# A new order in the k, v and r projections of an RWKV-7 / attention decoder, and a new beginning of its scan

## The chip, the cores and the metric

The kernel runs on one core of a Trainium2 chip. The metric is the device time of one execution in microseconds (us). Its engines are TensorE (PE; PEld is its weight load), VectorE (DVE), ScalarE (ACT), GpSimd (POOL) and SyncE (SP, which here only issues DMAs). Each runs its own instructions in program order; between engines there are semaphores only.

## What is computed

One step of a two-layer decoder trunk: 1024 prompt tokens and 8 sample tokens (1032 columns), model width 1024, 16 heads of 64. Layer 0 is an RWKV-7 mixer with its MLP, layer 1 windowed attention with its MLP. The change is in layer 0's mixer:

```
xr, xk, xv = h + (prev - h) * mix[...]           # prev: h one token earlier
r, k, v = xr @ w_r, xk @ w_k, xv @ w_v
kk = k * k_k, normalised per head;  k = k * (1 + (a - 1) * k_a)
state = state * w_t + (state @ a_t) b_t + v_t k_t   # a_t = -kk, b_t = kk * a; per token and head
y = state @ r_t;  bonus = sum(r * k * r_k) * v
```

The decay w and the gates a and g come from a stage before (scr_L, scr_A, scr_G in device memory).

## The kernel before, in words

Everything is stored channel-first: 8 row blocks of 128 channels by 1032 columns. The scan works on chunks of C = 64 tokens (16 chunks), so the projections also prepare, per chunk and head, the scaled rows At, Bt, Kt, Rt and the inverse T of a triangular system M.

**stage_kvr** makes k, v, r in 24 panels p of 128 output channels: k is p 0 to 7, v 8 to 15 (V0 = 8), r 16 to 23 (R0 = 16). A weight panel is loaded by SP (`weights`), rounded to a high part on ACT (`high`, L2052) and split on POOL (`wL`, L1891). PE then does, for each of 3 column slots, 8 row blocks times three products (high-high, low-high, high-low; L2015 to L2017): 72 matmuls of 344 columns. Panels 7, 8, 15 and 16 run `by_block` (L2031), row block outermost, since the operand changes there from x_k to x_v and from x_v to x_r: as soon as block b has been used (`s_used`), ACT may overwrite its high part (`used`, L1397), DVE its low part (`low`, L1401; `s_lo`). The mixed operand itself (`Blend`) is made ahead, one of 16 blocks at a time: `load` (ACT's DMA queue; it waits for mix b−2), `keep` (ACT, L1384), `mix` (DVE, L1392 and L1393). Between its slots PE does small work (`between`): for k block q the per-head sums of squares (`squares`, L1906) after slot 0 of panel q+1 and the systems (L1918) after slot 1 of panel q+2; for v the transposes to token order (`turn`, L1932, L1934), which ACT copies (`turned`, L2107, L2109) and SP stores; for r the bonus sums (`sums`, L1944).

The order of ACT within panel p is written out: square, high of the next panel, decays, keep, inverse_root (L2090, L2092), the loads, turned, then `copies` (L2061 for k, L2067 for v), which free PE's accumulators for the next panel. DVE does for k block q chain_a (needs scr_A's block, loaded by `load_A` on SP), chain_b, chain_c (at(q) is its last result), and the mask of q−1 (L2234); then the forward substitution of the 32 by 32 corners of all systems, two halves g of 30 steps with two instructions each (`forward`, L2246, L2248), with some mixes set between the steps (`aside`); then the 8 blocks of r (`scaled`, L2267; `bonus`, L2281) and the transposed corners (`turn_corners`, L2259). PE finishes T in panels 20 to 22 (`left` L1963, `right` L1975). SP issues in its own written order: in panel p weights of p+2, the three stores of k block p−1 (L1746 to L1750), L of p+1 (L1741), A of p (L1735), M of p−2 (L1754); later M by rows into the solve, T out and back in (`load_X`), and for r a store, the wait for its landing and the next load, for two buffers (`load_rL`, `load_rV`). `first_chunks` loads part of the scan's first operands (BK0, W0). The stage ends when SP has seen all its stores land; then comes a barrier of all engines.

**stage_scan** starts by loading AR (At and Rt of two chunks), Z (the T's) and W (values) on SP. PE turns the sample columns (`smp.turn`), ACT copies and stores them and loads them back by head (`spread`, `vectors`), DVE clears Y, ysq and Yt (2048, 512 and 2048 columns). Then come `grams` (L2566), `by_token` (L2582), `values_in`, and the 16 chunks of about 10 us each.

## Time and profile before

| | us |
|---|---|
| median of 3 runs | 2873.45 |
| lowest, highest | 2868.9, 2877.31 |
| the profiled execution | 2874.99 |
| its span in the profile | 2873.2 |
| PE, DVE, ACT, POOL busy | 2642.3, 1204.4, 961.9, 544.3 |

The profile is of one execution. PE is busy for 92% of its span. Matmuls are pipelined, so their busy times overlap and their starts tell the pace. A row of the timeline begins with start and duration; in brackets stands the time for which the engine was idle before, and what released it.

### The profile page before, as it was taken

What the parts mean: (1) busy time and instruction counts of PE and PEld (TensorE: products, weight loads), DVE (VectorE), ACT (ScalarE), POOL (GpSimd) and SP (SyncE); (2) the same over time, 40 slices, a digit from 0 to 9 for tenths busy, and PEclk for the clock granted to TensorE, in tenths of its full rate; (3) what the DMA queues carried; (4) which work ended last, traced back from release to release, by engine and by line L of the source; (5) the groups of instructions that cost most, each with busy time, mean ns of one, the idle gap of its engine ahead of it and who ended that gap; (6) DMA issues with size and microseconds to landing.
All of it is one profiled execution on the core that took longest, in us unless ns stands there. A gap on an engine that the chain in (4) does not pass through costs nothing. (4 is left out here: it accounts for less than half of the span.)

```text
span 2873.2 us, 48859 instructions
## 1 busy us (share of the span) xinstructions
PE 2642.3 (92%) x20648; PEld 2487.2 (87%) x20648; DVE 1204.4 (42%) x2171; ACT 961.9 (33%) x1817; POOL 544.3 (19%) x347
## 2 busy tenths in 40 slices
PE   4989878989958999999999999897999999999998
PEld 2768768878858899999999998786989999999998
DVE  5346686249967421211212252666562122121223
ACT  4446523324435421311202343556442021130221
POOL 1121211103330112121221312110212222222230
PEclk7999989989978999999999999999899999999999
DMA  8867659788673122222222222211211111111121
GB/s 321 325 238 236 206 192 266 202 210 194 168 234 94 59 89 88 74 88 89 74 88 89 87 76 71 65 28 39 84 42 51 45 45 52 45 45 52 45 67 60
DMA packets 375329, 332.04 MB, mean 116 GB/s; under 512 B 105688, under 2 KB 344988, under 8 KB 368046
## 3 DMA queue, kind: packets, MB, share of 16 engines
q1 hardware_dynamic: 353404, 288.22, 33.4%
q10 hardware_dynamic: 15986, 20.69, 2.3%
q0 software_dynamic: 5728, 20.06, 1.9%
...
q14 instruction: 47, 0.39, 0.0%
...
## 5 line engine op out<-in xcount | busy, mean ns | idle before, releaser
L531 POOL TENSOR_TENSOR wL<-raw,wH 128x1024 fp32r<-128x1024 f32 x120 | 288.0, 2400 | 1298.7 <-ACT wH L655 1298.7
L552 PE MATMUL t_acc<-oneH,wH 128*128 128x344 f32 x1488 | 483.5, 325 | 11.8 <-DVE oneL L899 5.8
L554 PE MATMUL t_acc<-oneH,wL 128*128 128x344 f32 x1488 | 478.4, 321 | 0.0
L553 PE MATMUL t_acc<-oneL,wH 128*128 128x344 f32 x1488 | 478.0, 321 | 0.0
L552 PE MATMUL t_acc<-twoH,wH 128*128 128x344 f32 x1392 | 449.2, 323 | 7.0 <-DVE twoL L874 4.8
L554 PE MATMUL t_acc<-twoH,wL 128*128 128x344 f32 x1392 | 445.9, 320 | 0.0
L553 PE MATMUL t_acc<-twoL,wH 128*128 128x344 f32 x1392 | 445.4, 320 | 0.0
L824 DVE SCALAR_TENSOR_TENSOR X<-t_acc,mod,X 128x344 f32<-128x344 f32 (+1 forms) x240 | 137.5, 573 | 615.7 <-PE t_acc L554 594.3
L904 DVE TENSOR_TENSOR t_g<-t_g 128x344 f32<-128x344 f32 x192 | 99.4, 518 | 553.2 <-ACT t_g L675 553.2
L552 PEld LDWEIGHTS t_acc<-oneH,wH 128*128 128x128 f32 x1488 | 281.9, 189 | 26.1 <-issue 10.1
L655 ACT ACTIVATE wH<-raw 128x1024 fp32r<-128x1024 f32 x120 | 126.5, 1054 | 507.6 <-PE t_acc L554 507.6
L553 PEld LDWEIGHTS t_acc<-oneL,wH 128*128 128x128 f32 x1488 | 282.4, 190 | 0.6
L554 PEld LDWEIGHTS t_acc<-oneH,wL 128*128 128x128 f32 x1488 | 282.3, 190 | 0.0
L552 PEld LDWEIGHTS t_acc<-twoH,wH 128*128 128x128 f32 x1392 | 262.3, 188 | 20.0 <-issue 11.2
L553 PEld LDWEIGHTS t_acc<-twoL,wH 128*128 128x128 f32 x1392 | 262.7, 189 | 0.1
L554 PEld LDWEIGHTS t_acc<-twoH,wL 128*128 128x128 f32 x1392 | 262.6, 189 | 0.0
L675 ACT ACTIVATE t_g<-t_acc 128x344 f32<-128x344 f32 x192 | 87.8, 457 | 508.0 <-PE t_acc L554 508.0
L2015 PE MATMUL kvr_acc<-hxH,kvr_wH 128*128 128x344 f32 x480 | 162.5, 339 | 10.7 <-PEq L122 7.3
L2016 PE MATMUL kvr_acc<-hxL,kvr_wH 128*128 128x344 f32 x480 | 156.6, 326 | 0.0
L2017 PE MATMUL kvr_acc<-hxH,kvr_wL 128*128 128x344 f32 x480 | 156.5, 326 | 0.0
L552 PE MATMUL t_acc<-twoH,oneH 128*128 128x344 f32 x336 | 114.0, 339 | 30.6 <-DVE twoL L899 29.9
L1891 POOL TENSOR_TENSOR kvr_wL<-kvr_raw,kvr_wH 128x1024 fp32r<-128x1024 f32 x22 | 58.6, 2665 | 324.4 <-ACT kvr_wH L2052 324.4
...
## 6 DMA issues: line engine op xcount, KB each, us to landing
...
```

Source lines behind the costliest of these rows:

```text
L531: pool.tensor_tensor(low, raw_of(w), high.bitcast(F32), ALU.subtract).then_inc(s_low, 1)
L552: pe.matmul(out, high[:, k, :], h[:, k, third[t]], start=(k == 0), stop=False)
L553: pe.matmul(out, high[:, k, :], l[:, k, third[t]], start=False, stop=False)
L554: return pe.matmul(out, low[:, k, :], h[:, k, third[t]], start=False, stop=(k == DB - 1))
L655: act.activation(place(kind, p)[0], raw_of(w), ACT.Copy).then_inc(s_high, 1)
L675: act.activation(gsq[:, i % 3, :], acc[u % 4][:, 0:TT], ACT.Relu).then_inc(s_relu, 1)
L824: ins = dve.scalar_tensor_tensor(out=x, in0=acc[u % 4][:, 0:z - a], scalar=gate[:, m, 0:1], in1=x, op0=ALU.mult, op1=ALU.add)
L904: dve.tensor_tensor(x, x, x, ALU.mult).then_inc(s_g, 1)
L1891: pool.tensor_tensor(wL[:, p % 2], raw[:, p % 2], wH[:, p % 2].bitcast(F32), ALU.subtract).then_inc(s_low, 1)
L2015: pe.matmul(out, wH[:, s, b, :], net.HH[:, b, t], start=(b == 0), stop=False)
L2016: pe.matmul(out, wH[:, s, b, :], net.HL[:, b, t], start=False, stop=False)
L2017: ins = pe.matmul(out, wL[:, s, b, :], net.HH[:, b, t], start=False, stop=(b == DB - 1))
```

## The change

In stage_kvr: SP loads A of block p ahead of the stores of block p−1, and store_v ahead of the M loads; T goes out in panels 14 and 18 (before 13 and 15) and back in in 15 and 18 (before 14 and 16). POOL copies the sample columns ahead of the split. PE turns v block 0 in panel 10 (before in 9), block 1 in its third slot. ACT loads and keeps the blocks of x_r in pairs; of the high parts at a change of operand it does three ahead of the inverse root, three behind it and two behind the copies (before, seven ahead of the copies, or four and four). DVE mixes inside chain_a; mixes x_r blocks 0 and 1 ahead of the solve and the rest in it, makes all low parts of x_r after step 15 of its second half and `scaled(0)` after step 20; the corners are turned after scaled(1) and inside scaled(4).

For the scan: AR's first buffer AR0 lies where v lay in stage_kvr and is filled there, At by a DMA in first_chunks (now panels 19 to 23), Rt by one copy of 128 columns on DVE per block. The landings of the last stores of r, BV and T are waited for in the scan (`s_late`, `s_lateX`). The second AR buffer is loaded on ACT's queue. The scan begins with grams, by_token, grams, then the turn of the samples; POOL clears the buffers; `vectors` is on SP, in front of the second Z; the samples' state comes in four quarters of 512 KB, one for each group of four chunks, before in one load of 2 MB. Cut (renamings, places in memory and unchanged lines left out; numbers are lines before):

```diff
@@ 195
             net.W0 = first.enter_context(nc.sbuf_tensor("first_W", [128, 2, DB, HD], F32))
+        net.s_late, net.s_lateX = (nc.alloc_semaphore(name=n) for n in ("late", "late_X"))
@@ 1672
 R_AT = 15632
+with ExitStack() as first:
+    first.enter_context(nc.sbuf_tensor("kvr_below_AR", [128, 12416], F32))
+    net.AR_left = nc.sbuf_bytes_remaining
+    net.AR0 = first.enter_context(nc.sbuf_tensor("first_AR", [128, DB, 2, 2, C], F32))
@@ 1787
         sp.wait_ge(s_freeR, q * NT + NT)
-        sp.dma_start(net.sRt[q], rL[:, q % 2, :]).then_inc(s_rst[q % 2], 16)
+        sp.dma_start(net.sRt[q], rL[:, q % 2, :]).then_inc(s_rst[q % 2] if q < DB - 1 else net.s_late, 16)
...
         sp.wait_ge(s_bv, q * NT + NT)
-        sp.dma_start(net.sBV[q], rV[:, q % 2, :]).then_inc(s_bvst[q % 2], 16)
+        sp.dma_start(net.sBV[q], rV[:, q % 2, :]).then_inc(s_bvst[q % 2] if q < DB - 1 else net.s_late, 16)
...
             sp.wait_ge(s_vst, 16 * DB)
+            sp.wait_ge(s_t, 3 * DB)
+            for s in range(2):
+                sp.wait_ge(s_vcst[s], 16 * (DB // 2))
+            sp.dma_start(net.AR0[:, :, 0].rearrange("p b c t -> p b (c t)"), net.sAt[:, :, 0:2 * C].rearrange("b p t -> p b t")).then_inc(s_pre, 16)
@@ 1813
             x = ZX[r, j // 4, 0:C * C].rearrange("p (c t) -> p c t", t=C)[:, 16 * (j % 4):16 * (j % 4) + 16, 32:64]
-            sp.dma_start(net.sT[2 * j:2 * j + 2, :, r, 32:64].rearrange("c b p t -> p (c b) t"), x).then_inc(s_Xst, 16)
+            sp.dma_start(net.sT[2 * j:2 * j + 2, :, r, 32:64].rearrange("c b p t -> p (c b) t"), x).then_inc(net.s_lateX, 16)
@@ 1822
             weights(p + 2)
+        if 2 <= p < DB:
+            load_A(p)
...
                 load_L(p + 1)
-        if 2 <= p < DB:
-            load_A(p)
...
             store_M(p - 2)
+        if V0 < p <= V0 + DB:
+            store_v(p - V0 - 1)
@@ 1839
                 sp.dma_start(ZX[:, g, 0:C * C], by_row(net.sM)[g]).then_inc(s_Z[g], 16)
-        if V0 < p <= V0 + DB:
-            store_v(p - V0 - 1)
...
             store_tok(p - V0 - 2)
-        if p in (13, 15):
-            g = (p - 13) // 2
+        if p in (14, 18):
+            g = (p - 14) // 4
@@ 1867
                 load_rV(q + 1)
-        if 18 <= p < 23:
-            first_chunks(p - 18)
+        if p == 18:
+            load_X(1)
+        if 19 <= p:
+            first_chunks(p - 19)
...
     store_bv(DB - 1)
-    for x in (s_vcst, s_rst, s_bvst):
+    for x in (s_rst, s_bvst):
         for s in range(2):
-            sp.wait_ge(x[s], 16 * (DB // 2))
-    sp.wait_ge(s_vst, 16 * DB)
+            sp.wait_ge(x[s], 16 * (DB // 2 - s))
     sp.wait_ge(s_stokst, 16 * DB)
-    sp.wait_ge(s_Xst, 16 * 16)
-    sp.wait_ge(s_pre, 160)
+    sp.wait_ge(s_pre, 176)
...
     for p in range(2, NP):
-        pool.wait_ge(s_high, p - 1)
-        pool.tensor_tensor(wL[:, p % 2], raw[:, p % 2], wH[:, p % 2].bitcast(F32), ALU.subtract).then_inc(s_low, 1)
...
                 pool.tensor_copy(net.step_cols[:, q, i * DEC:(i + 1) * DEC], x).then_inc(s_cols, 1)
+        pool.wait_ge(s_high, p - 1)
+        pool.tensor_tensor(wL[:, p % 2], raw[:, p % 2], wH[:, p % 2].bitcast(F32), ALU.subtract).then_inc(s_low, 1)
@@ 1980
                 squares(p - 1)
-            elif V0 < p <= V0 + DB:
-                if p == V0 + 1:
-                    systems(DB - 1)
-                else:
-                    turn(p - V0 - 1)
+            elif p == V0 + 1:
+                systems(DB - 1)
+            elif V0 + 1 < p <= V0 + DB:
+                turn(p - V0 - 1 if p > V0 + 2 else 0)
...
             systems(p - 2)
-        if slot == 2 and p == V0 + 1:
-            turn(0)
+        if slot == 2 and p == V0 + 2:
+            turn(1)
@@ 2129
             high(p + 1)
-        if p == DB:
-            used(0, DB - 1)
-        if p == R0:
-            for b in range(4, DB):
-                used(1, b)
...
             blend.keep(act, p)
+        if p == DB - 1:
+            for b in range(3):
+                used(0, b)
...
             blend.load(act, p + 1)
-        if p in (8, 9):
+        if p in (8, 10, 12, 14):
             blend.load(act, p)
-        if 10 <= p <= 13:
-            blend.load(act, p)
-        if p == 12:
+            blend.load(act, p + 1)
+        if p == 11:
...
                 act.wait_ge(s_stK[s], 16 * (DB // 2))
-        if 9 <= p <= 13:
+        if p in (9, 11, 13, 15):
             blend.keep(act, p - 1)
-        if p == 14:
-            blend.load(act, 14)
-            blend.keep(act, 13)
+            blend.keep(act, p)
...
         if p == DB - 1:
-            for b in range(DB - 1):
+            for b in range(3, 6):
...
         if p == 15:
-            blend.load(act, 15)
-            blend.keep(act, 14)
-            blend.keep(act, 15)
-            for b in range(4):
+            for b in range(6):
@@ 2174
             copies(p)
+        if p in (DB - 1, 2 * DB - 1):
+            for b in range(6, DB):
+                used(p // DB, b)
@@ 2204
         n = own.mark(dve.tensor_tensor(x, x, k[:, s, :], ALU.mult))
+        if q < DB - 1:
+            blend.mix(dve, q)
+        if q == DB - 2:
+            blend.mix(dve, q + 1)
+        if q == DB - 1:
+            blend.low(dve, q)
@@ 2233
-    def forward(g, aside):
+    def forward(g, aside, lows=None, first=None):
@@ 2246
             dve.tensor_tensor(z[:, :, 0:s, s + 1:32], z[:, :, 0:s, s + 1:32], x, ALU.add).then_inc(s_z, 1)
-            if (g, s) in aside:
-                blend.mix(dve, DB + aside[g, s])
+            for b in aside.get((g, s), ()):
+                blend.mix(dve, DB + b)
+            if s == lows:
+                for b in range(DB):
+                    blend.low(dve, DB + b)
+            if s == first:
+                scaled(0)
@@ 2267
                 bonus(q - 1)
+            if n == 1 and q == 4:
+                turn_corners(1)
...
         dve.tensor_copy(net.step_cols[:, q, DEC:2 * DEC], rL[:, s, SEQ:TOK])
+        if q == 0:
+            dve.wait_ge(s_t, 3 * DB)
+            for i in range(2):
+                dve.wait_ge(s_vcst[i], 16 * (DB // 2))
+        dve.tensor_copy(net.AR0[:, q, 1].rearrange("p c t -> p (c t)"), rL[:, s, 0:2 * C])
@@ 2282
         n = chain_a(q)
-        if q < DB - 1:
-            blend.mix(dve, q)
+        chain_b(q, n)
+        if q == DB - 1:
+            mask(q - 1)
+        chain_c(q)
         if q == DB - 2:
-            blend.mix(dve, q + 1)
-        if q == DB - 1:
-            blend.low(dve, q)
-        chain_b(q, n)
-        chain_c(q)
-        if q:
+            for b in range(2):
+                blend.low(dve, b)
+        if 0 < q < DB - 1:
...
         if q == DB - 2:
-            for b in range(DB - 1):
+            for b in range(2, DB - 1):
...
     mask(DB - 1)
-    forward(0, {(0, 10): 0, (0, 22): 1})
-    forward(1, {(1, 4): 2, (1, 14): 3, (1, 24): 4})
-    for b in range(5, DB):
+    for b in range(2):
         blend.mix(dve, DB + b)
-    for b in range(DB):
-        blend.low(dve, DB + b)
-    for q in range(DB):
+    forward(0, {(0, 8): [2], (0, 9): [3], (0, 24): [4], (0, 25): [5]})
+    forward(1, {(1, 12): [6], (1, 13): [7]}, 15, 20)
+    for q in range(1, DB):
         scaled(q)
-        if q in (0, 2):
-            turn_corners(q // 2)
+        if q == 1:
+            turn_corners(0)
@@ 2348
-def vectors(self, act):
-    act.wait_ge(self.s_rows, 16)
+def vectors(self, sp):
+    sp.wait_ge(self.s_rows, 16)
     for i in range(5):
-        act.dma_start(self.vec[:, i, :], self.net.sSmp[i].rearrange("s (h d) -> (s h) d", d=HD)).then_inc(self.s_vec, 16)
-    act.dma_start(self.S[:], self.net.io["state_wkv"][0].rearrange("s h i j -> (s h) i j")).then_inc(self.s_S, 16)
+        sp.dma_start(self.vec[:, i, :], self.net.sSmp[i].rearrange("s (h d) -> (s h) d", d=HD)).then_inc(self.s_vec, 16)
+def state(self, sp, i):
+    rows = HD // 4
+    sp.dma_start(self.S[:, bass.ds(i * rows, rows), :], self.net.io["state_wkv"][0][:, :, bass.ds(i * rows, rows), :].rearrange("s h i j -> (s h) i j")).then_inc(self.s_S, 16)
@@ 2444
-AR = sb("AR", [128, 2, DB, 2, 2, C])
+net.sems += [net.s_late, net.s_lateX]
+AR = [net.AR0, sb("AR1", [128, DB, 2, 2, C])]
...
 S, U = sb("S", [128, DB, HD]), sb("U", [128, DB, HD])
+Y = sb("Y", [128, BODY, Q, 128])
+Yt = sb("Yt", [128, 2, DB, 2, C])
+St = sb("St", [HD, DB, 128])
...
 BK = [net.BK0, sb("BK1", [128, DB, 2, 2 * C])]
-Y = sb("Y", [128, BODY, Q, 128])
...
 ym, yv, yi = (sb(n, [128, Q * 2]) for n in ("ym", "yv", "yi"))
-Yt = sb("Yt", [128, 2, DB, 2, C])
-St = sb("St", [HD, DB, 128])
...
 pT = quarters(pSA)
-two_banks = [quarters(p) for p in (pU, pY)]
+two_banks = [quarters(p) for p in (pSA, pD)]
 smp = Samples(net, ctx)
+sb("below_AR", [128, (nc.sbuf_bytes_remaining - net.AR_left) // 4])
+sb("place_AR", [128, DB * 4 * C])
@@ 2478
 LOADS, LOADS_V = 10, 5
-loaded = lambda s, i: (s_ld[s], 16 * (LOADS * (i + 1) - (8 if s == 0 else 0)))
+loaded = lambda s, i: (s_ld[s], 16 * LOADS * (i + s))
@@ 2498
             eng.dma_start(W[s][c][at(1 - h), h], rows[h]).then_inc(s_ldV[s], 16)
+def columns(eng, two, s):
+    t = bass.ds(two * 2 * C, 2 * C)
+    for n, src in enumerate((net.sAt, net.sRt)):
+        eng.dma_start(AR[s][:, :, n].rearrange("p b c t -> p b (c t)"), src[:, :, t].rearrange("b p t -> p b t")).then_inc(s_ld[s], 16)
@@ 2508
             sp.wait_ge(s_G, two * 4 - 4)
-        t = bass.ds(two * 2 * C, 2 * C)
...
                     sp.dma_start(BK[s][at(h), :, c, at(n ^ h)], src[:, at(h), bass.ds(two * 2 * C + c * C, C)].rearrange("b p t -> p b t")).then_inc(s_ld[s], 16)
-        sp.wait_ge(s_Y, two * 2 + 1)
-        for n, src in enumerate((net.sAt, net.sRt)):
-            sp.dma_start(AR[:, s, :, n].rearrange("p b c t -> p b (c t)"), src[:, :, t].rearrange("b p t -> p b t")).then_inc(s_ld[s], 16)
+        if not first:
+            sp.wait_ge(s_Y, two * 2 + 1)
+            columns(sp, two, s)
+        elif s == 1:
+            smp.vectors(sp)
...
+    sp.wait_ge(net.s_lateX, 16 * 16)
...
         load(0, s, True)
+        if s == 0:
+            smp.state(sp, 0)
...
             load(i, s, False)
+            if s == 0:
+                sp.wait_ge(smp.s_S, i * 16)
+                smp.state(sp, i)
@@ 2554
+    for buf in (ysq, Y, Yt):
+        pool.memset(buf[:], 0.0).then_inc(s_ydv, 1)
+    pool.wait_ge(s_ydv, 4)
+    pool.sem_inc(s_yz, 1)
@@ 2644
+    grams(0, 0, 0, 0)
+    by_token(0, 0)
+    grams(0, 0, 0, 1)
     smp.turn(pe, two_banks)
-    for half in range(2):
-        grams(0, 0, 0, half)
-    by_token(0, 0)
+    pe.wait_ge(s_Gev, 6)
+    values_in(0)
     pe.wait_ge(s_yz, 1)
-    pe.wait_ge(s_Gev, 6)
-    pe.wait_ge(smp.s_tev, 2)
-    values_in(0)
@@ 2667
 def _(act):
-    smp.spread(act, two_banks)
-    smp.vectors(act)
+    act.wait_ge(net.s_late, 32)
+    columns(act, 1, 1)
@@ 2708
     by_token(0, 0)
+    smp.spread(act, two_banks)
@@ 2730
     dve.sem_inc(s_Y, Y0)
-    for n, buf in enumerate((Y, ysq, Yt)):
-        dve.memset(buf[:], 0.0).then_inc(s_ydv, 1)
     dve.memset(yv[:], 1.0).then_inc(s_ydv, 1)
-    dve.wait_ge(s_ydv, 4)
-    dve.sem_inc(s_yz, 1)
@@ 2767
             dve.tensor_tensor(S[:, b], S[:, b], net.pend[:, b, bass.ds(c, 1)].to_broadcast([128, 4, HD]), ALU.mult).then_inc(s_S, 1)
-        dve.wait_ge(smp.s_S, 16)
+        dve.wait_ge(smp.s_S, i * 16 + 16)
@@ 2792
         masked(0, 0, half)
+    dve.wait_ge(s_yz, 1)
...
         inverse(NCH + k)
```

## Rows read from the trace of the kernel before

**Rows 1.** The page, busy tenths in 40 slices of the span: TensorE.
```profile
PE   4989878989958999999999999897999999999998
```

**Rows 2.** Busy us of each engine by stage; granted clock, DMA share, GB/s.
```profile
192.00:303.00 111.00, 104.61 (x861) 97.59 (x862) 65.06 (x76) 70.94 (x89) 18.33 (x21) 0.98 0.72 227
303.00:327.00 24.00, 15.49 (x142) 14.32 (x142) 17.86 (x21) 17.68 (x21) 2.77 (x4) 0.90 0.66 211
327.00:486.00 159.00, 128.09 (x857) 124.39 (x858) 112.45 (x168) 54.95 (x86) 28.83 (x15) 0.89 0.72 219
486.00:603.00 117.00, 113.52 (x1569) 106.05 (x1567) 40.54 (x61) 31.54 (x45) 15.44 (x6) 0.97 0.75 205
```

**Rows 3.** What PE waited for, 190 to 640 us: total, times, longest.
```profile
PE kvr_pM L1932 <- ACT kvr_work L2109: 26.9, 3, 17.2
```

**Rows 4.** Timeline of PE (start us, us, line, tiles): check sums of k.
```profile
222.44 2.01 PE L1906 MATMUL kvr_ps<-kvr_work,const 128*128 128x344 f32 x6 [0.28 <-ACT kvr_work L2073]
237.85 1.90 PE L1906 MATMUL kvr_ps<-kvr_work,const 128*128 128x344 f32 x6
...
307.27 1.90 PE L1906 MATMUL kvr_ps<-kvr_work,const 128*128 128x344 f32 x6
```

**Rows 5.** Timeline, k panel 4: SP's issue of A, DVE's wait for it.
```profile
253.61 0.86 SPq L1735 DMA_DIRECT2D kvr_work<-scr_A  x1
...
259.86 0.82 DVE L2203 TENSOR_SCALAR kvr_work<-kvr_work,param,kvr_omka 128x1032 f32<-128x1032 f32 x1 [6.08 <-DMA kvr_work<-scr_A]
```

**Rows 6.** Timeline of PE and ACT at panels 7 and 8.
```profile
302.91 0.72 PE L2031 MATMUL kvr_acc<-hxH,kvr_wH 128*128 128x344 f32 x3 [1.81 <-ACT kvr_work L2061]
...
325.98 1.12 ACT L2061 ACTIVATE kvr_work<-kvr_acc 128x344 f32<-128x344 f32 x3
327.36 1.20 PE L2031 MATMUL kvr_acc<-hxH,kvr_wH 128*128 128x344 f32 x3 [8.86 <-ACT kvr_work L2061]
```

**Rows 7.** Timeline, v panel 10: DVE, ACT, PE.
```profile
377.04 1.28 DVE L1392 SCALAR_TENSOR_TENSOR kvr_xm<-kvrb_hx,param,kvr_xm 128x1024 f32<-128x1024 f32 x1
378.86 1.16 ACT L1384 ACTIVATE kvr_xm<-kvrb_hx,omix 128x1032 f32<-128x1032 f32 x1 [18.18 <-DVE kvr_xm L1393]
381.27 1.94 PE L1932 MATMUL kvr_pM<-const,kvr_work 128*128 128x128 f32 x8 [17.24 <-ACT kvr_work L2109]
```

**Rows 8.** Timeline of PE, panels 9, 12, 13 and 17.
```profile
345.45 0.39 PE L2015 MATMUL kvr_acc<-hxH,kvr_wH 128*128 128x344 f32 x1 [0.32 <-ACT kvr_work L2067]
...
414.66 1.07 PE L1932 MATMUL kvr_pM<-const,kvr_work 128*128 128x128 f32 x8
...
427.13 1.06 PE L1932 MATMUL kvr_pM<-const,kvr_work 128*128 128x128 f32 x8
...
485.48 0.39 PE L2015 MATMUL kvr_acc<-hxH,kvr_wH 128*128 128x344 f32 x1 [0.46 <-DVE kvr_work L2267]
```

**Rows 9.** Timeline of DVE: first and last step of the forward solve (120).
```profile
367.81 0.22 DVE L2246 TENSOR_TENSOR kvr_work<-kvr_work 128x60 f32<-128x60 f32 x1 [12.39 <-DMA kvr_work<-scr_M]
...
446.59 0.26 DVE L2248 TENSOR_TENSOR kvr_work<-kvr_work 128x60 f32<-128x60 f32 x1
```

**Rows 10.** Timeline of POOL and DVE during a split.
```profile
412.44 2.60 POOL L1891 TENSOR_TENSOR kvr_wL<-kvr_raw,kvr_wH 128x1024 fp32r<-128x1024 f32 x1 [15.86 <-ACT kvr_wH L2052]
412.82 2.64 DVE L2246 TENSOR_TENSOR kvr_work<-kvr_work 128x396 f32<-128x396 f32 x1
```

**Rows 11.** What SP waited for, 186 to 640 us: total, times, longest.
```profile
SPq L1879 <- DMA scr_BV<-kvr_work: 2.4, 1, 2.4
```

**Rows 12.** Timeline of PE at the scan's beginning.
```profile
619.78 2.08 PE L2566 MATMUL c_pG<-c_AR,first_BK 64*128 64x128 f32 x16 [4.57 <-DMA c_AR<-scr_Rt]
...
627.16 1.65 PE L2566 MATMUL c_pU<-first_W,c_Gm 64*64 64x64 f32 x26
```

**Rows 13.** Timeline of SP in the r panels: stores of Rt.
```profile
523.60 1.55 SPq L1790 DMA_DIRECT2D scr_Rt<-kvr_work  x1
...
542.30 1.54 SPq L1790 DMA_DIRECT2D scr_Rt<-kvr_work  x1
```

12 lines of the change are left out of this document (6 added, 6 removed).

## Prediction

> **What bounds the kernel now.** The page's slices come first: TensorE (PE) is busy 92% of the 2873.2 us span, and its digit is 9 in most slices from the 13th on [rows 1]; nothing of this change runs there. The gaps to look for are in slices 3 to 12 (190 to 850 us). A table by stage comes next [rows 2]: the 24 panels of the projections (three matrices k, v, r of eight column panels each) lie from 192 to 603 us, and PE is not busy in 6.4 of the 111 us of k panels 0 to 6, in 8.5 of 24 us at panel 7 and the handover, in 31 of 159 us in panels 8 to 16, and in 3.5 of 117 us in panels 17 to 23. Then the list of what PE waited for: first 26.9 us for ACT's copy of the turned v blocks (L2109) [rows 3]. The timeline gives each wait its place and its cause, below: 8.86 for ACT's copy of k [rows 6] and 4.57 for scr_Rt at the scan's start [rows 12] among them. PE is the bound between these gaps: a v panel without a wait takes 427.13 − 414.66 = 12.5 us [rows 8]; without its turn (1.07) that is 11.4 for 72 matmuls, 0.158 each, 1.42 for the nine of a row block, 3.8 for a slot of 24.
>
> **The change, part by part.**
>
> *A. load_A in front of store_k.* From panel 2's check sums to panel 3's are 237.85 − 222.44 = 15.4 us with no wait between; the next four panels, to 307.27, take 69.4, 17.4 each [rows 4]. Cause: SP queues the load of A(q) behind store_k(q−1), so it is issued at 253.61, after at(q−1), and DVE stands 6.08 us until 259.86 [rows 5]. Now it needs only the systems of q−2, which PE ends 7.8 us behind the check sums of q−1, where the old issue comes 253.61 − 237.85 = 15.8 us behind them, and PE becomes the bound. Worth 69.4 − 4 × 15.4 − 0.5 (panel 7 makes its check sums after three row blocks, 4.3, not after 3.8) = 7.3 us. Below: a transfer landing late gives 0 back; worse than nothing is bounded by one extra 6 us landing behind the two bigger queues, −6. I take 6, near the upper end, since A is now issued some 8 us earlier and needs to come only 6 earlier. SP sleeps in load_A until slot 1 of the panel while Kt waits to be stored; that delays a store no one needs within the panel. The step columns taken ahead of the split on POOL are three copies of 8 columns, and the split has a panel's slack: 0. The mix in chain_a now lies under DVE's wait for the squares: within the 15.4.
>
> *B. Handover k to v.* Panel 7 ends at 327.36 − 8.86 = 318.5; ACT then makes seven high parts (about 0.98 each) and only then, at 325.98, the copies, and PE starts panel 8 at 327.36 with the clock down: the first three matmuls take 1.20 where they take 0.72 elsewhere, and the first four triples cost about 1.7 more [rows 6]. In the change three high parts come before the inverse root, three behind it, both under panel 7, and the copies stand before the last two. Worth 8.86 + 1.7 = 10.6. New waits: the three copies, 1.1 us, now end the wait for panel 8, as they must; the copies of panel 8 stand behind the later inverse root of q=7, about 1 us. The low parts on DVE (1.17 us each) keep ahead of PE's 1.4 per block. I take 9; bounds 5 and 10.6.
>
> *C. v panels.* PE's 17.24 us at 381.27: turned(0) stands on ACT behind blend.load(10), which waits for mix 8, and that sits in the forward solve on DVE after step 10: DVE mixes at 377.04, ACT, idle for 18.18 us, issues the load and keeps at 378.86, copies the turned tiles at 379.93, and PE goes on [rows 7]. The same at 400.62 (4.23) and 445.06 (5.39). After each the granted clock must rise again (0.89 over this stretch [rows 2]): the eight transposes take 1.94 instead of 1.07, and twelve matmuls start 0.29 apart instead of 0.158: 2.5 us after the long wait, some 1.4 and 2 after the others [rows 7, 8]. Now mixes 8 and 9 stand before the solve, loads go in pairs two panels ahead of their mixes, and panel 9's turn moves to panel 10, where it has its copies inside. From panel 9 to 17, 345.45 to 485.48, is 140.0 us [rows 8]. PE's own work: panel 9 with the systems 14.4; panel 10 with two turns 13.6; five at 12.5; panel 16 with its turn 12.6: 103.1. New small waits: where ACT does a high part (1.05), two keeps (2.3) and turned (1.3) after the copies of a panel (0.5), 5.2 us, and PE asks for it after a slot of 3.8: 1.4 each in panels 11, 13 and 15; 1.1 for the copies before panel 16; up to 1 at 17, where DVE has scaled(0). 6.3 in all. 140.0 − 109.4 = 30.6; I take 30.
>
> The cover of this is the solve. Its 120 ops run from 367.81 to 446.85, 79 us, five mixes inside [rows 9]. In the change it starts where the M loads land: A and B bring panel 9 to about 330; systems(7), the mask, store_M (355.44 to 359.42) and the load (to 367.81 [rows 9]), 12.4 us together, put the start at 350. Six mixes inside, three short stalls for keeps, bring it to step 15 of the second half at about 422; then eight low parts, and panel 16, due at 425, begins on the first of them. Step 20's scaled(0) waits for panel 16 on purpose, and ten steps (9 to 11 us) follow before scaled(1), which PE needs when panel 17 ends: slack 0 to 2 us. Upper bound of C: all 26.9 + 5.9 ramps + 3.4 waits before 16 and 17 = 36. Lower: the solve late by 20 us and its wait with PE, 10.
>
> At one point a rule bears on the slack. DVE's step at 412.82 takes 2.64 us where its neighbour takes 0.57, and POOL's split runs from 412.44 for 2.60 [rows 10]: each split may cost the solve 2.07 us, five fall in it, and I have counted them. The Trainium skill (SBUF — State Buffer, "Who interferes with whom") says that a DVE instruction with two SBUF inputs excludes a GpSimd one that reads SBUF, and that one which only writes does not. By that rule the trace agrees for the splits, and POOL's new memsets in the scan's beginning would hold nobody up; no row here shows a memset beside DVE's masks.
>
> *D. End of the stage and the scan's beginning.* SP stores the last BV at 608.96 and waits 2.4 us for its landing [rows 11], a wait that moves to ACT of the scan: −2.4. The scan starts at 613.35; grams at 619.78 when scr_Rt lands, values_in at 627.16, 13.8 us after the start [rows 12]. With AR0 in place grams start once DVE has cleared yv and S, about 1.5 us in. From the durations: grams 2.1 [rows 12], by_token 2.0 beside the mask 1.3, grams 2.1, turn 2.0, mask done: values_in at 9.7, and chunk 0 at 11.4 instead of 15.2: −3.8. The three memsets are 4608 columns, 4.0 us on DVE (1.76 for 2048); on POOL, even at twice that, they end before values_in. Z has 11 + 3 us to land, where the two loads of the table took 6 to 10. Sum 6.2; the vectors for the sample step stand now in SP's queue ahead of Z(1): up to 2 us back. I take 5; bounds 0 and 8.
>
> *E. r panels.* The tensor_copy to AR0 is eight times 0.17 us like the neighbouring copy of 8 columns, or more (128 columns): on DVE, idle 3 to 8 us per panel. turn_corners moves (4.63 us of DVE for two) to panels 17 and 20; left(0) and left(4) need them at 20 and 21. I take 0; from −2 to a loss of 11 (first rival).
>
> Sum: 6 + 9 + 30 + 5 + 0 = 50 us. Against the profiled execution (2874.99, span 2873.2, 1.8 us around it): 2825.0. That execution is 1.5 us over the median 2873.45, which I leave in: about 2825.
>
> **Rivals.**
>
> *1. The transfers take it back: 2842.* For it: DMA is at 0.72 to 0.75 of its time in all these stages [rows 2]; the k panels' bytes in 15.4 instead of 17.6 us bring it near 0.9. SP's own loop in the r panels (store, wait for landing, load; twice) has a pitch of 542.30 − 523.60 = 18.7 us already [rows 13]. The change puts into it the 2 MB store of T(1), some 11 us (466.59 to the X load behind it at 477.71), and AR0's load, 6 (613.82 to 619.78 [rows 12]). Slack: DVE's scaled(3) at 518.97 against the start of PE's panel 20 near 525, 6 us. 17 − 6 = 11 lost, and A's 6 not gained: 2842. Against it: r panels 20 to 22 are longer on PE than on SP.
>
> *2. The solve comes late: 2837.* If splits hit the solve's steps and mixes six more times, 12 us, minus the slack of 2, wait before panel 16 or 18: 2825 + 10, and 2 more for a clock ramp. For it: the slack is thin. Against it: it starts 18 us sooner.
>
> *3. Slower than before: the r panels fall to SP's pace: 2888.* Place: SP's two landings per r panel. Price: if T(1), X(1) and A0 stretch both from 7 to 13 us, the pitch goes from 18.7 to 31 against PE's mean of 117/7 = 16.8: 7 × 14 = 98, less 35 of slack in panels 20 to 22 (three of about 20 us, entered ahead), 63: 2825 + 63 = 2888. It decides from a round trip above about 10 us; before, it is 6.8 and 8.1 in the same panel.
>
> *4. Nothing moves: 2870.* ACT stays behind some other wait (the landing of the tok stores, s_vst) in the same places. Against it: at 378.49 the load's issue itself is what comes late [rows 7].
>
> **Chances and range.** Forecast 0.70 (2811 to 2835 by the bounds of A to E), rival 1 0.14, rival 2 0.09, rival 3 0.04, rival 4 0.03. The range reaches over rivals 1 and 2: 2812 to 2848. A change of 0.3% (9 us) is what can be told from none here; faster 0.93, within 0.03, slower 0.04.
>
> **What would show it.** In the profile after: PE's wait for L2109 falls from 26.9 to under 6 us; the squares of panels 3 to 6 come 15 to 16 us apart; the wait of 8.86 becomes 1 to 2; panel 17 starts near 440 (before 485.48), the scan near 565, its chunk 0 11 to 12 us later. Wrong would be: waits of PE for hxL or for scaled before panels 16 to 18 over 3 us in sum, a stretch of panels 17 to 23 longer than 120 us, or an A load that lands after DVE is free.

## The result and the profile after

The changed kernel takes 2843.4 us (median of 4 runs, 2837.43 to 2847.88) against 2873.07 (4 runs) for the kernel before on the same chip: ratio 0.9891, 95% interval 0.9874 to 0.9907. That is faster by about 30 us where 48 were forecast; it lies in the range, 1.4 us from rival 1. The profiled execution took 2839.51 us, span 2837.7, granted clock 0.965.

TensorE's line of the page after, in 40 slices of 71 us. Against [rows 1] the fifth to seventh (284 to 497 us) rise from 8, 7, 8 to 9, 9, 9, and the eighth falls from 9 to 8; the 9 and 5 of the eleventh and twelfth are 7 and 7 because the gap at the scan's tail now begins 31 us earlier (816.74 to 785.74):
```profile
PE   4989999889779999999999998997999999999998
```
The busy table of the stages after (columns as in [rows 2]; the bounds follow the panels, which now come earlier):
```profile
194.00:299.00 105.00, 103.43 (x862) 97.88 (x863) 80.54 (x79) 71.36 (x90) 20.80 (x22) 0.98 0.79 247
299.00:320.00 21.00, 18.25 (x154) 17.12 (x153) 19.17 (x19) 20.91 (x27) 6.08 (x8) 0.94 0.73 230
320.00:449.00 129.00, 118.14 (x844) 115.09 (x842) 101.00 (x144) 51.47 (x80) 25.34 (x12) 0.97 0.78 245
449.00:582.00 133.00, 117.36 (x1570) 109.95 (x1570) 54.59 (x94) 31.69 (x45) 14.97 (x6) 0.92 0.74 205
```
PE is idle 1.6 us in k panels 0 to 6 (6.4 before), 2.8 at panel 7, 11 in the v panels (31 before), and 16 in the r panels, where it was 3.5: the first three stages gave, the fourth took. What PE waited for, 194 to 600 us (total, times, longest), where [rows 3] had 26.9 us for one cause:
```profile
PE kvr_pM L1984 <- ACT kvr_work L2124: 9.7, 1, 9.7
...
PE kvr_pM L1941 <- ACT kvr_work L2117: 6.3, 2, 5.3
...
PE kvr_ps L1953 <- DVE kvr_work L2294: 3.4, 2, 2.1
PE kvr_acc L2039 <- DVE hxL L1402: 2.7, 1, 2.7
```
The new 9.7 is one wait in panel 20. Here is its history in the timeline (start us, us; SPq and ACTq are issues of DMAs on that engine's queue). SP:
```profile
468.87 0.57 SPq L1858 DMA_DIRECT2D scr_T<-kvr_work  x1
469.49 0.43 SPq L1795 DMA_DIRECT2D scr_Rt<-kvr_work  x1
480.76 0.33 SPq L1776 DMA_DIRECT2D kvr_work<-scr_L  x1
...
488.72 0.73 SPq L1791 DMA_DIRECT2D kvr_work<-scr_T  x1
489.50 11.27 SPq L1732 DMA_DIRECT2D kvr_raw<-in_rw_wr  x1
500.84 1.00 SPq L1795 DMA_DIRECT2D scr_Rt<-kvr_work  x1
506.50 0.32 SPq L1776 DMA_DIRECT2D kvr_work<-scr_L  x1
```
and ACT, PE behind it:
```profile
505.19 1.06 ACT L2060 ACTIVATE kvr_wH<-kvr_raw 128x1024 fp32r<-128x1024 f32 x1 [19.57 <-DMA kvr_raw<-in_rw_wr]
510.83 1.06 ACT L2174 ACTIVATE kvr_work<-kvr_work 128x1032 f32<-128x1032 f32 x1 [4.59 <-DMA kvr_work<-scr_L]
511.92 2.43 ACT L2124 ACTIVATE kvr_work<-kvr_pM 32x512 f32<-32x512 f32 x4
...
513.17 1.76 PE L1984 MATMUL kvr_pM<-kvr_work 32*32 32x32 f32 x58 [9.68 <-ACT kvr_work L2124]
```
Read it backwards. PE's right(0) needs left_out(0) on ACT (511.92). That copy's own input was there at about 500, but in ACT's order it stands behind the high part of panel 21 (505.19) and the exp of r block 4 (510.83). Both were late: the weights because their issue stood 11.27 us on SP behind the 2 MB load X(1), the exp because rL(4) waited for store_r(2), which was issued behind those weights. One step earlier the 2 MB store of T(1) stands in front of store_r(1), whose landing took 11.3 us (469.49 to 480.76). Behind this wait the granted clock is low (the third figure from the end of a row), and it falls once more in panel 21, where PE stands for 2.34 us without a releaser that the profile names:
```profile
509.00:521.00 12.00, 7.83 (x149) 7.77 (x150) 6.71 (x7) 5.76 (x9) 0.00 (x0) 0.58 0.90 230
521.00:533.00 12.00, 10.30 (x279) 9.08 (x278) 3.81 (x8) 5.65 (x8) 2.37 (x1) 0.98 0.68 205
533.00:539.00 6.00, 5.36 (x29) 5.29 (x29) 0.00 (x0) 1.18 (x2) 0.00 (x0) 0.50 0.87 171
```
```profile
533.64 0.53 PE L1972 MATMUL kvr_pM<-kvr_work 32*32 32x32 f32 x12 [2.34 <-issue]
```
From sums to sums of the r blocks, the loss lies in few places: 9.5 us in the interval that holds panel 20's wait (22.6 before, 32.1 after), and 1.3 in each of two others (block 0 to 1, block 4 to 5).

To compare kernels I cut the stretch from the first check sums of k to the scan's first grams at four points, which are starts of PE rows in the timelines: check sums of k block 6, of block 7, sums of r block 0, sums of r block 7 (before: 208.89, 307.27, 333.91, 489.80, 604.94, 619.78). All runs below, in us, each from its one profiled execution; "ratio" with its interval is from all timed runs against the kernel before:

```
                      k0-k6  k6-k7  k7-r0   r0-r7  r7-grams  all     median   ratio
before                98.4   26.6   155.9   115.1  14.8     410.9    2873.07
after                 91.6   19.9   131.7   127.4   5.6     376.2    2843.4  0.9891 [0.9874, 0.9907]
e4  A alone           91.6   20.5   158.6   112.8  14.6     398.0    2861.3  0.9960 [0.9945, 0.9975]
e12 two mixes ahead   98.6   27.0   142.7   114.4  14.1     396.8    2860.0  0.9946 [0.9932, 0.9961]
e2  M on ACT          91.6   18.8   132.3   129.6   6.3     378.5    2845.5  0.9902 [0.9888, 0.9916]
e9  M(1) later        91.6   18.6   129.2   120.8   9.9     370.1    2837.6  0.9878 [0.9858, 0.9897]
e1  T, X on ACT       91.6   19.6   130.7   121.8   5.6     369.3    2835.1  0.9870 [0.9856, 0.9885]
e3  e1 and e2         91.6   18.7   132.4   121.9   5.6     370.1    2839.7  0.9875 [0.9860, 0.9890]
e5  no T(1), X(1)     91.6   19.9   131.8   110.1  15.7     369.2    2835.4  (one run)
e7  left_out first    91.6   19.9   131.7   120.8   7.4     371.4    2842.5  0.9897 [0.9877, 0.9916]
e8  e1 and e7         91.6   19.8   132.6   113.2  12.2     369.3    2837.6  0.9874 [0.9857, 0.9891]
e10 e8, corners ACT   91.6   19.7   130.5   114.4   6.2     362.4    2832.7  0.9857 [0.9839, 0.9874]
e11 e10 and e9        91.6   19.6   132.1   111.1   6.8     361.2    2825.0  0.9825 [0.9811, 0.9838]
e13 memsets on DVE    91.6   19.8   132.2   128.9  12.4     384.9    2846.7  0.9896 [0.9872, 0.9920]
```
The timed runs of one kernel spread over 5 to 15 us, those of the kernel after over 10, so differences of a few us are read in the stretches and not in the medians. A stretch has a spread too. From squares(7) to sums(0) the seven kernels that have the same code there (after, e1, e5, e7, e8, e10, e13) took 130.5 to 132.6 us, and over the r panels after, e2 and e13, which are the same there, took 127.4 to 129.6. A difference of 2 us in one stretch decides nothing. Outside the whole stretch the profiled executions took 2460 to 2473 us; the medians hold that part as well.

### The profile page after: what moved, and what is told of

It reads as the page before. It is cut to its first block and busy times, and to the rows that moved or that the text cites. A ratio compares the mean times of both kernels' runs of the same rounds, so it can differ in the third digit from the quotient of the medians.

```text
span 2837.7 us, 48881 instructions
## 1 busy us (share of the span) xinstructions
PE 2633.7 (93%) x20648; PEld 2482.2 (87%) x20648; DVE 1219.8 (43%) x2176; ACT 962.3 (34%) x1817; POOL 550.0 (19%) x350
## 3 DMA queue, kind: packets, MB, share of 16 engines
q8 instruction: 164, 2.69, 0.4%
## 5 line engine op out<-in xcount | busy, mean ns | idle before, releaser
L553 PE MATMUL t_acc<-oneH,wH 128*128 128x344 f32 x1488 | 483.7, 325 | 12.2 <-DVE oneL L900 5.8
L554 PE MATMUL t_acc<-twoL,oneH 128*128 128x344 f32 x336 | 110.6, 329 | 0.0
```

The costliest lines, as they stand in the source:

```text
L553: pe.matmul(out, high[:, k, :], h[:, k, third[t]], start=(k == 0), stop=False)
L554: pe.matmul(out, high[:, k, :], l[:, k, third[t]], start=False, stop=False)
```

## Experiments

**Which parts of the gain are whose: A alone, C's core alone.** e4 is the kernel before with only
```
                     weights(p + 2)
+                if 2 <= p < DB:
+                    load_A(p)
                 if 1 <= p <= DB:
                     store_k(p - 1)
...
-                if 2 <= p < DB:
-                    load_A(p)
```


> The kernel before with one edit: SP's load of A(p) in front of the stores of k(p-1). Theory (the prediction's part A): the check sums of panels 3 to 6 come 15.3 to 15.5 us apart and not 17.4, the k panels 6 to 7 us shorter, nothing else changed in front of panel 7: 2866 to 2867 us. Rival: the k panels got their 7 us from the other edits (mix ahead of the maximum, step columns ahead of the split), and this edit alone gives under 2 us.

Measured: k0-k6 98.4 to 91.6, exactly as in the whole change; the rival is out. The whole is 2861.3 us, 5 below what I expected. But k6-k7, which I had booked on part B, also falls from 26.6 to 20.5, nearly to the 19.9 of the whole change. Panel 8's start in e4:
```profile
311.07 3.91 ACT L1397 ACTIVATE hxH<-kvr_work 128x1032 fp32r<-128x1032 f32 x4
314.88 1.12 ACT L2061 ACTIVATE kvr_work<-kvr_acc 128x344 f32<-128x344 f32 x3
...
316.26 0.71 PE L2031 MATMUL kvr_acc<-hxH,kvr_wH 128*128 128x344 f32 x3 [3.38 <-ACT kvr_work L2061]
```
ACT makes all seven high parts in front of the copies as before, but has its copies at 314.88 and not at 325.98: A of the last blocks is there in time, and the chain up to the inverse root runs ahead by that much. The wait is 3.38, not 8.86 [rows 6], and the matmuls take 0.71, not 1.20. So one edit of four lines gave some 13 of the 30 us (2861.3 against 2874.5 in the same runs).

e12 is the kernel before with mixes 8 and 9 taken out of the solve:
```
             mask(DB - 1)
-            forward(0, {(0, 10): 0, (0, 22): 1})
-            forward(1, {(1, 4): 2, (1, 14): 3, (1, 24): 4})
-            for b in range(5, DB):
+            for b in range(2):
+                blend.mix(dve, DB + b)
+            forward(0, {(0, 10): 2, (0, 22): 3})
+            forward(1, {(1, 4): 4, (1, 14): 5, (1, 24): 6})
+            for b in range(7, DB):
                 blend.mix(dve, DB + b)
```


> The kernel before with one edit on DVE: mixes 8 and 9 stand ahead of the forward solve and the five others of its inside each move up by two places. Nothing else. Theory (the prediction's part C, its core): the waits of 17.24, 4.23 and 5.39 us for the copies of the turned v blocks, and the ramps of the clock behind them, come from ACT's load of block 10 waiting for mix 8; they fall to under 8 us in sum, and squares(7) to sums(0), 155.9 us before, takes 130 to 135 us: 2849 to 2853. Rival: loads in pairs and the moved turn of panel 9 are needed for it, and the waits only move to other panels: 145 us or more.

Measured: 155.9 to 142.7, between the two, and 2860.0 us where 2849 to 2853 were expected. The waits for the turned tiles (26.9 us) are gone from PE's list altogether, so the cause was named rightly; but what comes next is late by more than I expected:
```profile
458.20 1.20 PE L2031 MATMUL kvr_acc<-hxH,kvr_wH 128*128 128x344 f32 x3 [14.27 <-DVE hxL L1401]
```
The solve still starts at 370.61 and ends at 455.19, and panel 16 waits for its low parts behind it. Here rival 2's mechanism decides. The earlier start of the solve and the low parts inside its second half are what the change adds; with A they make the other 11 us. That it is these two is read from the waits; no run takes them one by one.

**The v panels: queue or bandwidth?** In the kernel after, panel 11 waits 5.3 us, and behind it the transposes take 1.94 instead of 1.06. ACT had stood for weights that SP issued behind the two 2 MB loads of M:
```profile
367.22 1.06 ACT L2060 ACTIVATE kvr_wH<-kvr_raw 128x1024 fp32r<-128x1024 f32 x1 [5.16 <-DMA kvr_raw<-in_rw_wv]
...
371.64 1.94 PE L1941 MATMUL kvr_pM<-const,kvr_work 128*128 128x128 f32 x8 [5.30 <-ACT kvr_work L2117]
```
SP's issues:
```profile
350.93 0.81 SPq L1852 DMA_DIRECT2D kvr_work<-scr_M  x2
351.78 0.44 SPq L1732 DMA_DIRECT2D kvr_raw<-in_rw_wv  x1
352.27 9.35 SPq L1764 DMA_DIRECT2D scr_Vc<-kvr_work  x1
```
These weights were issued at 351.78, ahead of the issue that stood for 9.35 us, and landed 15.4 us later: it was their landing that was long, not their issue. e2 issues the M loads from ACT, behind its loads of blocks 10 and 11 and the same waits:
```
+                if p == 10:
+                    ...
+                    for g in range(2):
+                        act.dma_start(ZX[:, g, 0:C * C], by_row(net.sM)[g]).then_inc(s_Z[g], 16)
```


> The kernel after, with the two 2 MB loads of M issued by ACT at its panel 10 and not by SP. Panel 9 to panel 17 took 113.85 us. Theory 'queue': SP stood 9.35 us in the issue behind them, the weights of panel 12 landed late and PE waited 5.30 us for the turned tiles with a fall of the clock behind; now that wait falls below 1.5 us and the stretch takes 106 to 109 us; the panels 17 to 23 keep their 133 us. Rival 'bandwidth': the weights share the engines with the M loads from any queue, and high(12) still comes some 5 us late: 112 to 115 us.

Measured: 132.3, no gain (114.7 us from panel 9 to panel 17, as the rival had it). Of SP's stall of 9.35 one of 4.55 is left. The weights are in time, but SP now issues them at 348.19, ahead of the M loads at 352.99, and ACT waits at the same place for another transfer:
```profile
364.47 1.05 ACT L2053 ACTIVATE kvr_wH<-kvr_raw 128x1024 fp32r<-128x1024 f32 x1
...
371.96 1.08 ACT L2108 ACTIVATE kvr_work<-kvr_pM 128x512 f32<-128x512 f32 x2 [4.35 <-DMA scr_V<-kvr_work]
```
The store of v by token, issued on SP's queue at 357.67, landed at 371.96, 14 us later; the M loads on ACT's queue took 15.1 us to land (11.9 from SP). The rival was right here: 4 MB in one burst hold up the others from either queue. e9 splits the burst:
```
-                    for g in range(2):
-                        sp.dma_start(ZX[:, g, 0:C * C], by_row(net.sM)[g]).then_inc(s_Z[g], 16)
+                    sp.dma_start(ZX[:, 0, 0:C * C], by_row(net.sM)[0]).then_inc(s_Z[0], 16)
...
+                if p == 11:
+                    sp.dma_start(ZX[:, 1, 0:C * C], by_row(net.sM)[1]).then_inc(s_Z[1], 16)
```


> The kernel after with the second 2 MB load of M on SP some 20 us later (behind the weights of panel 13 and the tok stores of block 1); the forward solve needs it only near 405 us. With both loads on ACT's queue the wait at panel 11 stayed (4.5 us, now for the tok stores' landing), so not the queue but the 4 MB in one burst make it. Theory 'bandwidth': with half the burst the wait at panel 11 falls below 1.5 us and squares(7) to sums(0) takes 124 to 128 us, not 131.7; the second burst finds slack. Rival: the wait moves with the second load to panel 12 or 13: 130 to 133 us.

```profile
368.85 1.06 PE L1942 MATMUL kvr_pM<-const,kvr_work 128*128 128x128 f32 x8 [1.13 <-ACT kvr_work L2118]
```
The wait is 1.13 and the clock holds (the eight transposes take 1.06 and not 1.94); the stretch gives 2.6 us, which is 1.3 below the lowest of the seven equal runs. It ends 1.2 above the range I gave; panel 17 now waits 2.69 for scaled(0). The r panels gave another 6.6, which I had not expected. Of this 5.1 lie between the sums of blocks 4 and 5 (24.9 to 19.8), where the stand of 2.34 us and the second fall of the clock are missing. The wait before right(0) is still 8.51. The solve ended at 458.34 instead of 462.33; whether that is why the stand is gone is not shown.

**The r panels: SP's queue, the bytes, or ACT's order?** e1 moves T(1) and X(1) from SP to ACT, behind high(19) and high(20):
```
-                if p in (14, 18):
+                if p == 14:
...
-                if p == 18:
-                    load_X(1)
+                if p == 18:
+                    act.wait_ge(s_diag, 2)
+                    act.dma_start(by_row(net.sT)[1], ZX[:, 1, 0:C * C]).then_inc(s_zst[1], 16)
+                if p == 19:
+                    act.wait_ge(s_zst[1], 16)
+                    act.dma_start(...net.sT[8:16]...).then_inc(s_XT[1], 16)
```


> The kernel after, with the 2 MB store of T(1) and the 2 MB load X(1) issued by ACT (its panels 18 and 19) and not by SP. Panels 17 to 23 took 132.8 us in the kernel after (119.5 before). Theory 'queue': both stood in SP's one queue in front of store_r(1), load_rL(3), the weights of panel 21 and store_r(2), and SP's issue of the weights stood 11.27 us; without them the chain ends with slack again: 119 to 123 us, PE's wait of 9.68 us before right(0) gone, the whole 10 to 13 us faster than after. Rival 'bandwidth': the 16 DMA engines are full, and the same bytes delay the same transfers from any queue: 129 to 134 us. Rival 'solve': DVE's late end of the forward solve sets it: no change either, and the wait before right(0) stays above 7 us.

> Both edits together: M loads, T(1) and X(1) on ACT's queue. Theory 'queue': panels 9 to 23 take 17 to 20 us less than in the kernel after, the whole about 2825 us, what the prediction gave. Rival 'bandwidth': within 3 us of the kernel after, 2843. If only one of the two sites is a queue effect, it comes out between, as the single runs say.

Measured: 121.8 us from sums to sums, 5.5 less than after, and 2835.1 us, 8 less. In the measure of the expectation, from panel 17's start, it is 125.8 where after has 132.8: between 'queue' (119 to 123) and 'bandwidth' (129 to 134). e3 has the same 121.9 and nothing more, as e2 leads one to think (2839.7; 5.9 us less from panel 9 on, not 17 to 20). The issue behind X(1) is short again, but the load of rL(3), issued just behind X(1), takes 9.6 us to land, and PE still waits:
```profile
475.15 0.88 ACTq L2161 DMA_DIRECT2D kvr_work<-scr_T  x1
...
476.36 0.32 SPq L1776 DMA_DIRECT2D kvr_work<-scr_L  x1
...
485.98 1.07 ACT L2178 ACTIVATE kvr_work<-kvr_work 128x1032 f32<-128x1032 f32 x1 [9.84 <-DMA kvr_work<-scr_L]
...
503.37 1.75 PE L1982 MATMUL kvr_pM<-kvr_work 32*32 32x32 f32 x58 [3.75 <-ACT kvr_work L2122]
```
So both theories hold a part. e5 takes the two transfers away (the second half's corners are then not computed rightly):
```
-                    load_X(1)
+                    sp.dma_start(ZX[:, 1, 0:C], net.sT[0, 0]).then_inc(s_XT[1], 16)
```


> The kernel after without the two transfers in the r panels: T(1) isn't stored there (only at the very end of the stage), and X(1) is a load of 16 KB in place of 2 MB; the corners of the second half of T are therefore not computed from what they should be. Panel 17's check sums to the last ones took 115.1 us before (sums 489.80 to 604.94), 127.4 after (454.65 to 582.03), 121.8 with both transfers on ACT's queue. Theory: the two transfers are the whole loss, by queue and by bandwidth: 114 to 117 us and the wait before right(0) under 1 us. Rival: a part is due to the edits on DVE (solve, corners, AR0 copies) and to where the rV and A0 loads fall: then 119 to 122 us.

110.1 us, under both expectations: 17.3 less than after, more than the whole loss of 12.2, and the edits on DVE in the r panels cost nothing that shows. It is even 5.0 less than the kernel before, which stood twice there (0.97 us at 538.97 and 2.15 at 557.70, with granted clocks of 0.79 and 0.72 in the 6 us around them), where e5 does not; what ended these two stands is not shown. e5's time at the end, 15.7 us, holds the store of T(1), which was moved there (issued at 572.85). e7 leaves them and changes ACT's order:
```
+                if p == 20:
+                    left_out(0)
+                    left_out(1)
                 if p >= 1 and p + 1 < NP:
                     high(p + 1)
...
-                    if m == 0:
-                        left_out(0)
-                        left_out(1)
```


> The kernel after with one edit on ACT: in panel 20 the copies left_out(0) and left_out(1) stand ahead of high(21) and the exp of rL(4), not behind them. Transfers as in after. Theory 'order': PE's 9.68 us before right(0) is ACT's queue order, since the copies' own input was ready at 500 and PE has 8 us of panel 20 left to hide the late weights: the wait gone, up to 3 us given back at panel 21 or its sums, the clock kept: 6 to 9 us faster, 2834 to 2837. Rival 'late inputs': the weights of panel 21 and exp(4) are late for panel 21 itself, and PE stands as long one place later: within 2 us of after, 2843.

> Both: T(1) and X(1) issued by ACT (5.5 us shorter r panels when alone) and the copies of left ahead of high(21). Theory 'order' gives the 3.75 us that PE still waited there and the clock behind it: 117 to 119 us from sums to sums, about 2831. Rival 'late inputs': 121 to 122 us as with the transfers alone, 2835.

In e7 the 9.68 is gone, and 4.19 comes back at the sums in panel 21:
```profile
519.33 3.81 PE L1953 MATMUL kvr_ps<-kvr_work,const 128*128 128x344 f32 x6 [4.19 <-DVE kvr_work L2294]
```
The clock is not kept, though I had expected it: it is 0.50 from 520 to 532 us. The r panels take 120.8, 6.6 less: theory 'order' in the stretch, though the median (2842.5, where 2834 to 2837 were expected) does not show it; the profiled execution, 2835.37 us, was the fastest of six. With the transfers on ACT too (e8) the r panels take 113.2, less than I expected, with both transfers still made. The price was therefore mostly what stood behind the transfers: ACT's order (6.6 alone, 8.7 on top of e1) and SP's queue (5.5 alone, 7.6 on top of e7). Which of the two is the larger can't be told with a spread of 2 us. About 3 us are left for the bytes themselves (e8 against e5).

**And the end of the stage.** e8's median is no better than e1's. In e1, e5 and e8 the grams come at 369.2 to 369.3 us from the start, but for three reasons: e5 has the store of T(1) at its end; in e1 PE's last sums (571.80) and SP's last corner store (572.24) come together; in e8 the sums are ready at 565.76, and SP issues corner stores until 574.13. e10 takes the corner stores off SP too (ACT issues them in panels 22 and 23 and waits for them at its end); e11 adds e9's edit:
```
-                if p >= NP - 2:
-                    for j in range(4):
-                        store_X(4 * (p - NP + 2) + j)
+                if p >= NP - 2:
+                    for j in range(4 * (p - NP + 2), 4 * (p - NP + 2) + 4):
+                        act.wait_ge(s_Xev, 2 * j + 2)
+                        ...
```

> The kernel of the run before (left_out first, T(1) and X(1) on ACT), and the 16 stores of T's corners issued by ACT as well, not by SP. There the r panels took 113.2 us from sums to sums, but the scan's first grams came 12.2 us after the last sums (5.6 in the kernel after), with PE waiting 10.2 us: from the stage's start to the grams 369.3 us, and just so in the two other kernels whose r panels got shorter (369.2, 369.3), against 376.2 in after. Theory: SP's own loop at the end is the next bound; the corner stores cost its queue 4.9 and 4.6 us of issue ahead of the last stores of Rt: without them 6 to 7 us earlier, 362 to 364 us from the start to the grams, 2828 to 2831. Rival: the bound is the landing of the last stores and of W0, whoever issues the corners: 368 to 370 us, no change.

> The same with the second load of M 20 us later (that alone gave the kernel after 2.6 us between squares(7) and sums(0), and its scan began 6.1 us earlier). Theory: the gains add, 2.5 us on the run beside it: 359 to 362 us from the start to the grams, near the predicted 2825. Rival: the later forward solve (its waits of 2.7 us before panel 17 took over there) eats it: no change against the run beside it.

SP at the end of e8:
```profile
560.53 4.94 SPq L1825 DMA_DIRECT2D scr_T<-kvr_work  x8
...
569.50 4.63 SPq L1825 DMA_DIRECT2D scr_T<-kvr_work  x8
574.17 0.60 SPq L1795 DMA_DIRECT2D scr_Rt<-kvr_work  x1
...
576.99 0.39 SPq L2555 DMA_DIRECT2D c_Z<-scr_T  x1
```
e8's last sums were at 565.76 and its grams at 577.97; e10 has them 6.2 us apart and 362.4 from the start, the 7 us expected; its median, 2832.7, is 1.7 above the range expected. e11 adds the later M(1): 2825.0 us (2821.65 to 2826.14), ratio 0.9825, the fastest of the series and the only one whose interval lies wholly below that of the changed kernel (e10's ends where that begins). Within its stretches it is only 1.2 us shorter than e10 (361.2, in the range expected), less than equal runs differ, so that they do not decide between the theory and its rival. PE now waits 6.63 us for scaled(0), the solve being late as rival 2 has it:
```profile
447.84 0.63 PE L2019 MATMUL kvr_acc<-hxH,kvr_wH 128*128 128x344 f32 x1 [6.63 <-DVE kvr_work L2291]
```
How the medians of e10 and e11 come to differ by 7.7 us the stretches don't show. The profiled executions differ by 2.3 (2823.94 and 2821.65), and e10's was the fastest of its four.

**The memsets.** e13 puts them back on DVE:
```
-            for buf in (ysq, Y, Yt):
-                pool.memset(buf[:], 0.0).then_inc(s_ydv, 1)
+            for buf in (Y, ysq, Yt):
+                dve.memset(buf[:], 0.0).then_inc(s_ydv, 1)
```

> The kernel after with the three memsets of the scan's beginning (4608 columns) back on DVE, ahead of the memset of S. Prediction: they are 4.0 us that stood on DVE before the first grams: sums(7) to the first grams goes from 5.6 to 9.6 us. Rival: something else (a landing, PE's sequencer) sets the first grams and the memsets are hidden: 5.6 to 6.5 us.

Measured 12.4 us from the last sums to the grams against 5.6; 9.6 were expected. From DVE's first memset to the grams it is 5.4 us (594.80 to 600.24), in the kernel after 0.8 (586.83 to 587.66): 4.6 us for a price of 4.0. The other 2 lie ahead of it, in the sums and the stage's end.

## Why the prediction was right, and where it fell short

The verdict and the range held; the likeliest number, 2825, was 18 us too good. That the range held owes something to luck: 2843.4 lies outside the forecast's own 2811 to 2835 and inside the range only because this was drawn over rivals 1 and 2. Rival 1's 2842 is near for a partly wrong reason: it takes back A's 6 us, which came in full, and leaves C and D as forecast, where C fell short by 6 in the table and D gave 4 more. The prediction's own signs were mixed. The squares came 15 to 16 us apart, as told; PE's waits for the turned tiles were 6.3 in sum (under 6 told), its wait in front of panel 8 was 2.75 (1 to 2 told), panel 17 started at 449.25 (near 440 told) and panels 17 to 23 took 132.8 us, over the 120 that it called wrong.

Four of its figures don't follow from the traces. The upper end 2835 isn't what the lower bounds of A to E give: these add up to −2, that is 2877. The DMA share that a k panel of 15.4 us should have is 0.72 × 17.4 / 15.4 = 0.81, not "near 0.9"; it came out at 0.79. From panel 9's start to the solve's the rows have 22.4 us, not 20, so that the start was due at 352. And it counts five splits of POOL in the solve: the kernel before has four (394.11 to 437.39), the one after seven. By the steps:

*A, 6 forecast (7.3 worked out).* k0-k6 gave 6.8. Squares 225.02, 240.44, 255.75, 271.06, 286.38: 15.3 apart as worked out. The fear of a late landing, which took it down to 6, did not come true, at a DMA share of 0.79. The last interval, to block 6, took 16.7, not 15.9, which is what is missing to 7.3. What the step missed is that A also shortens panel 7: another 6.2 in e4.

*B, 9 forecast.* k6-k7 gave 6.8, of which A alone gives 6.2. The split of the high parts is thus worth under 1 us here, less than equal runs differ (18.6 to 19.9), with 3 us in front of panel 8 left: DVE's part was not checked. Its mix takes 3.42 us beside a split on POOL, the two mixes stand ahead of the maximum of the squares, and the first low part ends too late:
```profile
301.13 3.19 POOL L1906 TENSOR_TENSOR kvr_wL<-kvr_raw,kvr_wH 128x1024 fp32r<-128x1024 f32 x1 [1.77 <-ACT kvr_wH L2060]
...
301.99 3.42 DVE L1393 SCALAR_TENSOR_TENSOR kvr_work<-kvrb_hx,param,kvr_work 128x1024 f32<-128x1024 f32 x1
...
315.65 2.37 DVE L1402 TENSOR_TENSOR hxL<-kvr_xm,hxH 128x1032 fp32r<-128x1032 f32 x2
...
317.03 0.74 PE L2039 MATMUL kvr_acc<-hxH,kvr_wH 128*128 128x344 f32 x3 [2.75 <-DVE hxL L1402]
```
"The low parts keep ahead of PE's 1.4 per block" was true of their rate, not of their start.

*C, 30 forecast.* Panel 9 to panel 17 went from 140.0 to 113.85 (335.40 to 449.25): 26.2. The cause was right (e12), and of the expected small waits those at panels 13 to 17 came out at 0.98, 0.64, 1.14 and 1.79. What the sum mis-sized is the one at panel 11: 5.3 us and a clock ramp, where it had 1.4. I had priced the M loads as a landing for the solve, not as 4 MB that everything behind them must let by. They also landed later than I put them: the solve began at 360.57, not 350 (2.6 of this is that the whole stage began later in this execution, 211.47 against 208.89). The low parts of x_r began at 430.74, not 422; PE came later too, at 434.84, and did not wait for them.

*D, 5 forecast.* Last sums to the scan's tail gave 8.1; to the grams 9.2. By e13 the memsets would take back 4.6 of it. In the kernel before they cost nothing by themselves: DVE ended them at 618.34, and the grams waited for scr_Rt until 619.78. So this gain needs both edits: e13 has AR0 in place alone (12.4 us where the kernel before has 14.8); no run has the memsets alone. The masks on DVE take the same beside POOL's memsets as without them. Kernel after, then e13:
```profile
587.13 1.80 POOL L2596 MEMSET c_Y<- 128x2048 f32 x1
588.87 1.80 POOL L2596 MEMSET c_Yt<- 128x2048 f32 x1
...
589.78 1.29 DVE L2789 TENSOR_TENSOR c_Gm<-c_pG,const 128x512 f32<-128x512 f32 x2 [2.33 <-PE c_pG L2608]
```
```profile
602.37 1.29 DVE L2789 TENSOR_TENSOR c_Gm<-c_pG,const 128x512 f32<-128x512 f32 x2 [2.33 <-PE c_pG L2604]
```
The mask has but one input in SBUF. The Trainium skill ("SBUF — State Buffer", "Who interferes with whom") says that a DVE instruction with at most one SBUF input, outside the 2-port modes, does not contend with GpSimd. The runs agree, 1.29 us in both; its rule for two inputs beside a memset, which the prediction named, they do not test.

*E, 0 forecast.* This is the step that failed: "I take 0". The r panels lost 13.3 us from panel 17's start (119.5 to 132.8; 12.2 in the table). The number was in the text, as rival 1: 11 lost to T(1)'s store and A0's load. Its first half was right, and the pitch of SP's loop did rise, from 18.7 to 31.4 us in one round (469.49 to 500.84; 16 to 18 in the next three), but A's gain was not taken back. From A0's load on (514.32) the r panels lost only 1.3 us more. And the mechanism was longer than told: not only SP's round trip, but the load X(1), behind which an issue stands 11.27 us, and ACT's order, which hands a late weight to a copy that didn't need it. By the experiments these two have about equal shares. The long issue was there to be seen: the kernel before has the same two transfers in panels 15 and 16, and one behind X(1) as well:
```profile
477.71 0.73 SPq L1786 DMA_DIRECT2D kvr_work<-scr_T  x1
478.54 10.33 SPq L1782 DMA_DIRECT2D kvr_work<-scr_Vc  x1
```
A queue-by-queue walk through panels 18 to 20 with the two 2 MB transfers put in would have moved this rival's 11 into the sum, and the forecast to about 2836.

Together: 6.8 + 6.8 + 24.2 − 12.2 + 9.2 = 34.8 from the check sums to the grams (410.9 to 376.2, 34.7 before rounding). The profiled executions differ by 35.5 (2874.99 to 2839.51); the medians by 30, since the profiled one of after was 3.9 below its median and that of before 1.9 above.

Rival 3 (SP's pace, 2888) did not come, but its place is real: once the r panels are short, SP's last issues set the scan's beginning (e8 against e10).
